# Sparse attention at the end of a two-block kernel: index scores computed during the projections, keys chosen beside the value projection, tiles 1 and 0 taken in turn

## The chip, the cores and the metric

One NeuronCore of a Trainium2 chip runs the whole program. The metric is the device time of one execution in microseconds; the median of the runs is compared. The engines are TensorE (PE), VectorE (DVE), ScalarE (ACT), GpSimd (POOL) and SyncE (SP), each with its own queue in order; they meet by semaphores alone.

## The reference

512 tokens of width 1024 go through a first block (gated linear attention, spatial gating, a mixture of experts) and a second one (a state-space mixer, a dense feed-forward, a sparse attention, a dense feed-forward, all in fp32). The change lies in the sparse attention:

```python
q, k, v, qi, ki, wi = split(h @ w_in)           # 16 heads of 64; 8 index heads of 64
q, k = rope(rmsnorm(q)), rope(rmsnorm(k))
qi, ki = rope(qi), rope(rmsnorm(ki))
for each block of 128 queries:
    score = sum over index heads of relu(qi @ ki.T) * wi      # causal
    sel   = the 128 keys of highest score
    out   = softmax(q @ k[sel].T / 8, causal) @ v[sel]
return out @ w_o
```

## The kernel before, in words

Activations stand transposed (features on the partitions, 512 tokens along a row) in pages of one large tile, `arena`. A product with an fp32 weight matrix is three products of split parts: `weights_high_part` (ACT, line 695) rounds half a chunk of weights, `weights_low_part` (DVE, line 703) forms the difference, two sets of parts take turns, and PE (`by_columns`, `by_rows`, line 336) waits for the set it needs. One half chunk holds the weights of one column block of 128. PE writes eight PSUM banks in the fixed order of the list `JOBS_B`; a bank is reused when its reader has freed it.

**Projections.** `ROPED` lists 21 column blocks of 128: eight of queries (`dq`), eight of keys (`dk`), four of index queries (`dqi`), one of index keys (`dki`); a loop of 23 steps walks them, and two value blocks (`dv`) stand in its last two steps. In step s PE makes `pr{s}` (24 products), the sum of squares `pn{s-1}` (line 1317) if that block is normed, and the rotary product `rot{s-2}` (line 1325). ACT squares and copies the block (1760, 1761), takes the root (1767) and rounds weights two blocks ahead. DVE inverts the root (2509), scales the block (2512), forms the weight difference, multiplies the rotary product by the sine (2525) and adds it to the block (2528), which POOL has multiplied by the cosine (906). The helper `copied` waits for its own instruction and then frees the bank; `link` waits for its own instruction alone.

**Attention.** `PAIRS` lists 64 pairs of a tile t of 128 queries and a head h, tile after tile; tile t sees (t + 1) x 128 keys. In step s PE makes the logits of pair s (line 1363), turns the probabilities of pair s-3 (1343, transposes) and multiplies those of pair s-4 with the values (1355). DVE adds the mask and takes the minimum (2582), and inverts the row sum (2539); ACT takes the exponential (1779), copies the turned probabilities (1789) and scales the outputs (1798, twice for two heads). In heads 1 to 4 of a tile, two index products a step of the next tile are added (1371), with a ReLU on ACT (1818) and a weighted sum on DVE (2559, 2562); POOL masks the diagonal (912). In heads 5 to 15 DVE chooses the next tile's keys: 16 rounds of `max` (eight largest) and `match_replace` (2597, 2598), and then the mask (2600). When a tile is done, eight transposes (1334) bring its rows back. The output projection (`wo`) waits for all tiles.

The order of the work is written out by hand: `JOBS_B` for PE and the banks, and the loops of each engine's program for the rest.

## Time and profile before

| | us |
|---|---|
| median of three runs | 3180.33 (3180.3 to 3219.16) |
| the profiled execution | 3193.29 |
| its span | 3191.5 |
| PE, DVE, ACT, POOL busy | 2930.1, 1876.4, 1406.8, 217.7 |

The span is the time between the first and the last instruction that the profiler saw on the core. Busy is the sum of an engine's instructions; a busy PE can run at either of two clocks, 1.2 or 2.4 GHz, which the profile gives as a granted share of 0.50 or 1.00. In the page's 40 slices of the span the granted clock is 0.6 and 0.5 in the two slices from 2633 to 2713 us, which lie in the attention. The last column of a group says which engine's work ended most of its idle time. The product of two fp32 operands is two instructions in the trace, a transpose one.

### The profile page before, as it was taken

How to read it: one execution, taken by the hardware profiler on the slowest of the kernel's cores; microseconds unless marked ns; L12 is line 12 of the kernel's file. 1: busy time of each engine (PE TensorE's matmuls, PEld its weight loads, DVE VectorE, ACT ScalarE, POOL GpSimd, SP SyncE). 2: the span in 40 equal slices, each digit the busy share in tenths (PEclk: the TensorE clock that was granted, in tenths of full speed). 3: DMA queues.
4: the chain of work that ended last, by engine and by line, in shares of the span. 5: the costliest groups of instructions: out<-in, count | busy, mean ns of one | idle time of the engine just before them, and what ended most of it. 6: DMA issues, size and time to landing. Idle time of an engine off the chain costs nothing.

```text
span 3191.5 us, 35348 instructions
## 1 busy us (share of the span) xinstructions
PE 2930.1 (92%) x12584; PEld 2247.2 (70%) x12584; DVE 1876.4 (59%) x2157; ACT 1406.8 (44%) x1858; POOL 217.7 (7%) x167
## 2 busy tenths in 40 slices
PE   7999999985899999999984678999989999989998
PEld 2548878765677777777773466888867766768887
DVE  3436643564988888888887754333249567343322
ACT  2323323223677777777775233222133344332321
POOL 1100100003930000000001000000001100000000
PEclk8999989995999999999997889999999965999999
DMA  6921722313898989899992812222221200112221
GB/s 229 331 76 60 288 75 93 111 65 150 319 344 354 387 354 387 352 387 352 387 360 74 106 43 76 93 103 96 93 74 67 79 27 1 37 69 99 99 93 66
DMA packets 90799, 546.88 MB, mean 171 GB/s; under 512 B 9232, under 2 KB 18848, under 8 KB 32384
## 3 DMA queue, kind: packets, MB, share of 16 engines
q1 hardware_dynamic: 79584, 485.65, 41.0%
q0 software_dynamic: 10816, 59.58, 5.4%
q8 instruction: 72, 1.18, 0.2%
q14 instruction: 39, 0.32, 0.0%
q10 hardware_dynamic: 288, 0.15, 0.0%
HBM read 516.51 MB, written 41.42 MB: 175 GB/s over the span
## 4 chain that ended last, share of the span: by engine, by line
PE 71%; DVE 15%; issue 6%; DMA 4%; ACT 3%; POOL 1%; SPq 1%; DVEq 0%; ACTq 0%; PEldq 0%; POOLq 0%
PE bank L336 39%; PE bank L274 6%; PE bank L1124 4%; PE bank L1128 4%; PE bank L1127 4%; DVE expert_low L2196 4%; PE bank L1363 2%; DMA arena<-in_we_stream 2%; PE bank L1355 1%; ACT expert_high L1559 1%; DMA arena<-in_mod 1%; PE bank L1343 1%; PE bank L1108 1%; DVE arena L2298 1%; DVE expert_x_low L2281 1%
## 5 line engine op out<-in xcount | busy, mean ns | idle before, releaser
L2196 DVE TENSOR_TENSOR expert_low<-arena,expert_high 128x2048 fp32r<-128x2048 f32 x291 | 683.4, 2379 | 102.3 <-ACT expert_high L1559 84.1
L1559 ACT ACTIVATE expert_high<-arena 128x1024 fp32r<-128x1024 f32 x582 | 596.9, 1057 | 212.3 <-PE bank L1124 120.5
L336 PE MATMUL bank<-high_b,weight_parts 128*128 128x512 f32 x1872 | 592.9, 398 | 30.4 <-DVE low_b L2434 16.2
L703 DVE TENSOR_TENSOR weight_parts<-ring_pages,weight_parts 128x1024 fp32r<-128x1024 f32 x185 | 226.9, 1227 | 556.0 <-ACT weight_parts L695 555.4
L695 ACT ACTIVATE weight_parts<-ring_pages 128x1024 fp32r<-128x1024 f32 x185 | 196.0, 1060 | 590.4 <-PE bank L336 547.0
L336 PEld LDWEIGHTS bank<-high_b,weight_parts 128*128 128x128 f32 x1872 | 352.5, 190 | 121.9 <-issue 37.2
L336 PE MATMUL bank<-low_b,weight_parts 128*128 128x512 f32 x832 | 324.8, 390 | 0.0
L1124 PE MATMUL bank<-expert_high,expert_x_low 128*128 128x512 f32 x768 | 309.4, 403 | 13.5 <-DVE expert_low L2196 9.9
L1127 PE MATMUL bank<-expert_high,expert_x_high 128*128 128x512 f32 x768 | 300.9, 392 | 0.0
L1128 PE MATMUL bank<-expert_low,expert_x_high 128*128 128x512 f32 x768 | 300.5, 391 | 0.0
L336 PE MATMUL bank<-hidden_parts,weight_parts 128*128 128x512 f32 x1056 | 240.0, 389 | 4.3 <-DVE hidden_parts L2480 4.3
L336 PEld LDWEIGHTS bank<-hidden_parts,weight_parts 128*128 128x128 f32 x1056 | 198.1, 188 | 46.3 <-DVE hidden_parts L2480 5.2
L336 PE MATMUL bank<-high_x,parts_a 128*128 128x512 f32 x640 | 204.6, 402 | 10.4 <-DVE parts_a L703 9.9
L1124 PEld LDWEIGHTS bank<-expert_high,expert_x_low 128*128 128x128 f32 x768 | 144.7, 188 | 68.3 <-DVE expert_low L2196 37.9
L336 PEld LDWEIGHTS bank<-low_b,weight_parts 128*128 128x128 f32 x832 | 156.8, 188 | 32.7
L1124 PE MATMUL bank<-expert_high,expert_h_low 128*128 128x512 f32 x384 | 156.2, 407 | 17.5 <-DVE expert_low L2196 15.1
L1128 PEld LDWEIGHTS bank<-expert_low,expert_x_high 128*128 128x128 f32 x768 | 144.8, 188 | 31.6
L1127 PEld LDWEIGHTS bank<-expert_high,expert_x_high 128*128 128x128 f32 x768 | 144.9, 189 | 28.0
L1128 PE MATMUL bank<-expert_low,expert_h_high 128*128 128x512 f32 x384 | 150.3, 391 | 0.0
L1127 PE MATMUL bank<-expert_high,expert_h_high 128*128 128x512 f32 x384 | 150.1, 391 | 0.0
L336 PEld LDWEIGHTS bank<-high_x,parts_a 128*128 128x128 f32 x640 | 123.2, 194 | 37.8 <-issue 11.1
L336 PE MATMUL bank<-high_b,parts_a 128*128 128x512 f32 x320 | 127.8, 399 | 0.0
(457 smaller groups left out, 4113.6 us busy)
## 6 DMA issues: line engine op xcount, KB each, us to landing
arena<-in_we_stream SPq DMA_DIRECT2D x294, 1024.0 KB, 6.4
ring_pages<-in_wb_stream SPq DMA_DIRECT2D x93, 1024.0 KB, 4.8
ring_pages<-in_wa_stream SPq DMA_DIRECT2D x49, 1024.0 KB, 4.8
arena<-in_mod POOLq DMA_DIRECT2D x16, 1024.0 KB, 6.7
xbuf<-arena POOLq DMA_DIRECT2D x25, 512.0 KB, 15.9
arena<-xbuf SPq DMA_DIRECT2D x17, 512.0 KB, 7.3
ybuf<-arena SPq DMA_DIRECT2D x16, 512.0 KB, 2.6
arena<-kd SPq DMA_DIRECT2D x8, 512.0 KB, 22.1
```

Of the source, the lines that this page charges most:

```text
L274: ins = pe.matmul(o, lhsT, rhs, start=start, stop=stop)
L336: ins = pe.matmul(o, lhsT, rhs, start=start, stop=stop)
L695: nc.scalar.activation(high, src, ACT.Copy).then_inc(weights_high, 1)
L703: nc.vector.tensor_tensor(low, src, high.bitcast(F32), ALU.subtract).then_inc(weights_split, 1)
L1108: ins = pe.transpose(ps[:, q * P:(q + 1) * P], parts[:, q * P:(q + 1) * P], ident[:])
L1124: ins = pe.matmul(o, low, w_high, start=start, stop=False)
L1127: pe.matmul(o, high, w_high, start=False, stop=False)
L1128: return pe.matmul(o, high, w_low, start=False, stop=stop)
L1343: ins = pe.transpose(ps[:, b * P:(b + 1) * P], pp[:, k % 4, b * P:(b + 1) * P], ident[:])
L1363: pe.matmul(ps[:, 0:(t + 1) * P], qT[r:r + 64, h // 2, t * P:(t + 1) * P], kT[r:r + 64, h // 2, 0:(t + 1) * P], start=True, stop=True).the ...
L1559: nc.scalar.activation(ehigh[c % HIGH_E][:, at], ring_e[c % RING_E][:, at], ACT.Copy) \
L2196: nc.vector.tensor_tensor(elow[c % RING_E][:], ring_e[c % RING_E], ehigh[c % HIGH_E][:].bitcast(F32), ALU.subtract).then_inc(weights_split ...
```

## The change

- `dqi` and `dki` come first in `ROPED` and in the weight stream. From step 8 (`INDEX_FIRST`) to step 19 each projection step has two index products behind `pr{s}`, two ReLUs on ACT ahead of the root, and two score instructions on DVE at the end of its step. The head weights (`wip`, `wi`) are made in steps 5 and 6. Scores of each tile stand in that tile's own `bias` page.
- DVE no longer adds the rotary parts; it writes the sine product to one of two pages (`rt`), and POOL does product and addition. POOL masks a tile's diagonal inside the same loop.
- The 48 rounds of choosing are spread: one in each of steps 13, 15, 17 and 19, sixteen and twelve beside the two value blocks (four or three behind each of four weight differences), and one in every third attention step up to step 47.
- `PAIRS` takes two heads of tile 1 and two of tile 0 in turn (numbers from 0), 32 steps, then tile 2, then tile 3. PE no longer waits for all rotated blocks before the first logits, but for the block that a pair needs.
- ACT no longer scales the outputs: DVE inverts two row sums at once and scales two heads in one instruction (`outputs_scaled`).
- In the first six attention steps PE makes one more product, `fill{s}`, whose result nobody reads, and waits for its end; before the first it waits for all value rows.

```diff
-            ("dq", "col", 0, 8), ("dk", "col", 0, 8), ("dqi", "col", 0, 4), ("dki", "col", 0, 1),
+            ("dqi", "col", 0, 4), ("dki", "col", 0, 1), ("dq", "col", 0, 8), ("dk", "col", 0, 8),
...
-ROPED = [("dq", j, True, 0) for j in range(KT)] + [("dk", j, True, 1) for j in range(KT)]
-ROPED += [("dqi", j, False, None) for j in range(4)] + [("dki", 0, True, None)]
+ROPED = [("dqi", j, False, None) for j in range(4)] + [("dki", 0, True, None)]
+INDEX_FIRST = len(ROPED) + 3
+ROPED += [("dq", j, True, 0) for j in range(KT)] + [("dk", j, True, 1) for j in range(KT)]
 NR = len(ROPED)
+INDEXED = [(t, i) for t in range(1, NTX) for i in range(IH)]
+
+
+def indexed_at(s):
+
+    return INDEXED[2 * (s - INDEX_FIRST):2 * (s - INDEX_FIRST) + 2] if s >= INDEX_FIRST else []
...
-PAIRS = [(t, h) for t in range(NTX) for h in range(AH)]
+assert sum(len(indexed_at(s)) for s in range(NR)) == len(INDEXED)
+
+PAIRS = []
+for _order in ((1, 0) * (AH // 2), (2,) * (AH // 2), (3,) * (AH // 2)):
+    for _n, _t in enumerate(_order):
+        PAIRS += [(_t, 2 * _order[:_n].count(_t) + i) for i in range(2)]
...
-NSTEP = NPAIR + MIX_LAG
...
+NSTEP, FILLED = NPAIR + MIX_LAG, 6
+TILE_DONE = {PAIRS.index((t, AH - 1)) + MIX_LAG: t for t in range(NTX)}
...
+            pool.wait_ge(S["b_bias0"], 1)
+            nc.gpsimd.affine_select(out=bias[0], in_=bias[0], compare_op=ALU.is_ge, fill=-MASKED, base=0,
+                                    pattern=[[-1, P]], channel_multiplier=1).then_inc(S["b_masked"], 1)
             for s in range(NR):
                 pool.wait_ge(bank_done, JB[f"rot{s}"] + 1)
                 v = roped_tile(s)
                 nc.gpsimd.tensor_tensor(v, v, cossin[:, 0, :], ALU.mult).then_inc(S["b_turned_cos"], 1)
-            pool.wait_ge(S["b_bias0"], 1)
-            nc.gpsimd.affine_select(out=bias[0][:, 0:P], in_=bias[0][:, 0:P], compare_op=ALU.is_ge, fill=-MASKED, base=0,
-                                    pattern=[[-1, P]], channel_multiplier=1).then_inc(S["b_masked"], 1)
-            for t in range(1, NTX):
-                pool.wait_ge(S["b_score_ready"], t)
-                nc.gpsimd.affine_select(out=score[:, t * P:(t + 1) * P], in_=score[:, t * P:(t + 1) * P],
-                                        compare_op=ALU.is_ge, fill=MASKED, base=0, pattern=[[-1, P]],
-                                        channel_multiplier=1).then_inc(S["b_masked"], 1)
+                pool.wait_ge(S["b_turned_cos"], s + 1)
+                pool.wait_ge(S["b_turned_sin"], s + 1)
+                nc.gpsimd.tensor_tensor(v, v, rt[:, s % 2, :], ALU.add).then_inc(S["b_rotated"], 1)
+                for t in range(1, NTX):
+                    if s < NR and (t, IH - 1) in indexed_at(s):
+                        pool.wait_ge(S["b_score_ready"], t)
+                        diagonal = bias[t][:, t * P:(t + 1) * P]
+                        nc.gpsimd.affine_select(out=diagonal, in_=diagonal, compare_op=ALU.is_ge, fill=MASKED, base=0,
+                                                pattern=[[-1, P]], channel_multiplier=1).then_inc(S["b_masked"], 1)
...
+                    for n, (t, i) in enumerate(indexed_at(s)):
+                        if s == INDEX_FIRST and n == 0:
+                            pe.wait_ge(S["b_rotated"], INDEX_FIRST - 3)
+                        ps = opened(f"ix{t}{i}")
+                        r = 64 * (i % 2)
+                        pe.matmul(ps[:, 0:(t + 1) * P], qiT[r:r + 64, i // 2, t * P:(t + 1) * P],
+                                  kiT[r:r + 64, 0:(t + 1) * P], start=True, stop=True).then_inc(bank_done, 1)
+                    if s == 5:
...
-            pe.wait_ge(S["b_rotated"], 2 * KT)
...
+                    pe.wait_ge(S["b_rotated"], NR - KT + h // 2 + 1)
...
-                    if t < NTX - 1:
-                        if s == 1:
-                            pe.wait_ge(S["b_rotated"], NR)
-                        for i in index_heads(h):
-                            ps = opened(f"ix{t + 1}{i}")
-                            r = 64 * (i % 2)
-                            pe.matmul(ps[:, 0:(t + 2) * P], qiT[r:r + 64, i // 2, (t + 1) * P:(t + 2) * P],
-                                      kiT[r:r + 64, 0:(t + 2) * P], start=True, stop=True).then_inc(bank_done, 1)
+                if s < FILLED:
+                    if s == 0:
+                        pe.wait_ge(S["b_v_rows"], 2 * NTX)
+                    ps = opened(f"fill{s}")
+                    pe.matmul(ps[:], ident[:], vt[:, 0, 0:512], start=True, stop=True).then_inc(bank_done, 1)
+                    pe.wait_ge(bank_done, JB[f"fill{s}"] + 1)
+                    pe.sem_inc(free(f"fill{s}"), 1)
...
+                    for t, i in indexed_at(s):
+                        ps = result(act, f"ix{t}{i}")
+                        if n_relu >= 2:
+                            act.wait_ge(relu_used, n_relu - 1)
+                        n_relu += 1
+                        copied(act, nc.scalar.activation(rl[:, i % 2, 0:(t + 1) * P], ps[:, 0:(t + 1) * P],
+                                                         ACT.Relu), S["b_relu_ready"], n_relu, f"ix{t}{i}")
...
-                if VALUE_LAG <= s < NPAIR + VALUE_LAG and (s - VALUE_LAG) % 2 == 1:
-                    k = s - VALUE_LAG
-                    name = f"av{k - 1}"
-                    act.wait_ge(av_done, k // 2 + 1)
-                    act.wait_ge(S["b_sums_ready"], k + 1)
-                    for n in (k - 1, k):
-                        t, h = PAIRS[n]
-                        ins = nc.scalar.activation(mixed_rows[t % 2][:, h * HD:(h + 1) * HD],
-                                                   psum[JB[name] % 8][:, h % 2 * HD:(h % 2 + 1) * HD], ACT.Copy,
-                                                   scale=rsm[:, n % 8:n % 8 + 1])
-                        ins.then_inc(S["b_o_ready"], 1)
-                    act.wait_ge(S["b_o_ready"], k + 1)
-                    act.sem_inc(free(name), 1)
...
+            def index_score(t, i):
+
+                n = IH * (t - 1) + i + 1
+                w = (t + 1) * P
+                dve.wait_ge(S["b_relu_ready"], n)
+                if i == 0:
+                    ins = nc.vector.tensor_scalar(bias[t], rl[:, i % 2, 0:w], wi[:, t, i:i + 1], None, ALU.mult)
+                else:
+                    ins = nc.vector.scalar_tensor_tensor(out=bias[t], in0=rl[:, i % 2, 0:w], scalar=wi[:, t, i:i + 1],
+                                                         in1=bias[t], op0=ALU.mult, op1=ALU.add)
+                ins.then_inc(relu_used, 1)
+                dve.wait_ge(relu_used, n)
+                if i == IH - 1:
+                    dve.sem_inc(S["b_score_ready"], 1)
+
+            chosen = [0]
+
+            def choose(n):
+
+                for _ in range(n):
+                    t, at = 1 + chosen[0] // (TOPK // 8), chosen[0] % (TOPK // 8)
+                    if t == NTX:
+                        return
+                    chosen[0] += 1
+                    if at == 0:
+                        dve.wait_ge(S["b_masked"], t + 1)
+                    link(nc.vector.max(m8[:], bias[t]))
+                    link(nc.vector.match_replace(bias[t], m8[:], bias[t], TAKEN))
+                    if at == TOPK // 8 - 1:
+                        link(nc.vector.tensor_scalar(bias[t], bias[t], TAKEN / 2, -MASKED, ALU.is_gt, ALU.mult))
+
             for s in range(NR + 2):
-                if s == NR + 1:
-                    ps = result(dve, "wi")
-                    link(nc.vector.tensor_scalar(wi, ps[:, 0:NTX * IH].rearrange("p (t h) -> p t h", h=IH),
-                                                 float(IH) ** -0.5, float(HD) ** -0.5, ALU.mult, ALU.mult))
-                    dve.sem_inc(free("wi"), 1)
                 if s >= NR:
-                    weights_low_part(dve, half_of("dv", s - NR, KT, True) + 1, split_to)
+                    for q in range(4):
+                        weights_low_part(dve, half_of("dv", s - NR, KT, True) - 2 + q, split_to)
+                        choose(4 if s == NR else 3)
...
+                    if s >= 4:
+                        dve.wait_ge(S["b_rotated"], s - 3)
+                    copied(dve, nc.vector.tensor_tensor(rt[:, s % 2, :], ps[:], cossin[:, 1, :], ALU.mult),
+                           S["b_turned_sin"], s - 1, name)
...
+                    for t, i in indexed_at(s):
+                        index_score(t, i)
+                    if s >= INDEX_FIRST + 5 and s % 2:
+                        choose(1)
...
+            def outputs_scaled(k):
+
+                t, h = PAIRS[k - 1]
+                name = f"av{k - 1}"
+                dve.wait_ge(S["b_exped"], k + 1)
+                link(nc.vector.reciprocal(rsm[:], sm[:, (k - 1) % 8:k % 8 + 1]))
+                dve.wait_ge(av_done, k // 2 + 1)
+                copied(dve, nc.vector.tensor_tensor(
+                    mixed_rows[t][:, h * HD:(h + 2) * HD].rearrange("p (h d) -> p h d", h=2),
+                    psum[JB[name] % 8][:, 0:2 * HD].rearrange("p (h d) -> p h d", h=2),
+                    rsm[:].unsqueeze(2).to_broadcast([P, 2, HD]), ALU.mult), S["b_o_ready"], k // 2 + 1, name)
...
+                if VALUE_LAG <= s < NPAIR + VALUE_LAG and (s - VALUE_LAG) % 2 == 1:
+                    outputs_scaled(s - VALUE_LAG)
+                if s in TILE_DONE:
+                    mixed_low(TILE_DONE[s])
+                if s < 3 * AH and s % 3 == 2:
+                    choose(1)
```

## Rows read from the trace of the kernel before

**Rows 1.** Stretches of the timeline: attention by tile, busy time of each engine, granted clock

```profile
2567.20:2598.00 30.80, 24.08 (x90) 15.94 (x88) 23.29 (x96) 17.03 (x64) 1.85 (x3) 0.65 0.05 22
2598.00:2646.30 48.30, 48.30 (x150) 31.86 (x151) 35.67 (x116) 24.03 (x79) 0.29 (x1) 0.50 0.00 1
2646.30:2700.70 54.40, 52.55 (x191) 33.79 (x189) 40.06 (x107) 27.00 (x74) 0.29 (x1) 0.63 0.00 1
2700.70:2749.60 48.90, 48.90 (x213) 31.83 (x214) 16.56 (x52) 24.30 (x63) 0.00 (x0) 0.77 0.00 1
2749.60:2758.90 9.30, 6.46 (x53) 5.72 (x53) 2.41 (x6) 4.88 (x13) 0.00 (x0) 1.00 0.00 0
```

**Rows 2.** The chain of waits in the projections: start, length, engine, line, pieces

```profile
2476.20 5.49 PE bank L336 x24
2481.69 0.86 PE bank L1317 x2
2482.55 0.86 PE bank L1325 x2
...
2521.54 21.79 PE bank L336 x96
```

**Rows 3.** Timeline of VectorE in one projection step: start, length, line, what

```profile
2469.36 3.35 DVE L2509 RECIPROCAL arena<-arena 128x512 f32<-128x512 f32 x1 [0.36 <-ACT arena L1767]
...
2473.53 1.23 DVE L703 TENSOR_TENSOR weight_parts<-ring_pages,weight_parts 128x1024 fp32r<-128x1024 f32 x1
2474.90 0.69 DVE L2525 TENSOR_TENSOR arena<-bank,arena 128x512 f32<-128x512 f32 x1
2475.74 0.69 DVE L2528 TENSOR_TENSOR arena<-arena 128x512 f32<-128x512 f32 x1
```

**Rows 4.** Groups of instructions in the attention: busy, mean ns, idle before, releaser

```profile
L1818 ACT ACTIVATE arena<-bank 128x512 f32<-128x512 f32 x8 | 4.8, 597 | 4.9 <-PE bank L1371 4.4 <-ACT arena L1818 0.4 <-ACT arena L1798 0.2
...
L2597 DVE MAX8 m<-arena 128x8 f32<-128x512 f32 x16 | 10.9, 682 | 0.3
...
L2562 DVE SCALAR_TENSOR_TENSOR arena<-arena 128x512 f32<-128x512 f32 x7 | 5.3, 752 | 2.4 <-ACT arena L1818 2.1
```

**Rows 5.** Groups of instructions in the projections: square root, GpSimd's product

```profile
L1767 ACT ACTIVATE arena<-bank,eps 128x512 f32<-128x512 f32 x17 | 11.7, 687 | 3.0 <-ACT arena L1761 2.2 <-PE bank L1317 0.5
...
L906 POOL TENSOR_TENSOR arena<-arena 128x512 f32<-128x512 f32 x20 | 26.6, 1330 | 170.7 <-PE bank L1325 170.7
```

**Rows 6.** Timeline of VectorE in tiles 0 and 1: logits and the next instruction

```profile
2580.74 0.29 DVE L2582 CUSTOM_DVE_ANT_0 arena<-bank,arena 128x128 f32<-128x128 f32 x1 [0.20 <-DVE arena L2598]
...
2581.19 0.16 DVE L2539 RECIPROCAL rsm<-sm 128x1 f32<-128x1 f32 x1
...
2621.25 0.42 DVE L2582 CUSTOM_DVE_ANT_0 arena<-bank,arena 128x256 f32<-128x256 f32 x1
...
2621.90 0.16 DVE L2539 RECIPROCAL rsm<-sm 128x1 f32<-128x1 f32 x1 [0.21 <-DVE nmx L2582]
```

**Rows 7.** Timelines of VectorE and GpSimd where they meet

```profile
2498.39 1.56 DVE L703 TENSOR_TENSOR weight_parts<-ring_pages,weight_parts 128x1024 fp32r<-128x1024 f32 x1 [0.67 <-ACT weight_parts L695]
...
2497.04 1.83 POOL L906 TENSOR_TENSOR arena<-arena 128x512 f32<-128x512 f32 x1 [5.04 <-PE bank L1325]
```

**Rows 8.** Stretches of tiles 1, 2 and 3, logit products alone: count, clock

```profile
2615.80:2643.30 27.50, 13.42 (x22) 5.49 (x22) 0.50 0.00 1
2673.00:2700.00 27.00, 12.12 (x15) 3.49 (x14) 0.50 0.00 1
2725.40:2749.80 24.40, 11.23 (x20) 2.94 (x20) 1.00 0.00 1
```

**Rows 9.** Timeline of PE: the last tile turned back

```profile
2755.91 1.09 PE L1334 MATMUL bank<-ident,arena 128*128 128x128 f32 x8 [0.61 <-ACT arena L1798]
```

**Rows 10.** Two stretches of 4 us at the high clock

```profile
2668.00:2672.00 4.00, 2.84 (x19) 1.98 (x17) 3.65 (x10) 1.60 (x5) 0.00 (x0) 1.00 0.00 0
2756.00:2760.00 4.00, 2.12 (x13) 1.71 (x14) 1.38 (x2) 1.61 (x3) 0.00 (x0) 1.00 0.00 0
```

More of the change, by code:

```diff
@@ L170 @@
         JOBS_B += [f"lg{_s}"]
-        if PAIRS[_s][0] < NTX - 1:
-            JOBS_B += [f"ix{PAIRS[_s][0] + 1}{i}" for i in index_heads(PAIRS[_s][1])]
+    if _s < FILLED:
+        JOBS_B += [f"fill{_s}"]
 JOBS_B += [f"wo{j}" for j in range(KT)] + ["sn4"]
@@ L641, in block_kernel @@
         cossin = page(31, 2, T)
-        bias = [page(32, T), page(43, T)]
-        score = page(32.5, T)
-        rl = page(33, 2, T)
+        bias = [page(first, (t + 1) * P) for t, first in enumerate((32, 37.75, 32.125, 32.5))]
+        rl = page(36, 2, T)
         pp = page(34, 4, T)
         pT = page(36, 2, T)
-        wi_rows = page(36.5, T)
+        wi_rows = page(34, T)
         rope = page(37.5, P)
         half1 = page(37.625, P)
-        mixed_rows = [page(42, D), page(43.5, D)]
+        mixed_rows = [page(first, D) for first in (42, 43.5, 42, 43.5)]
         sqt = page(42, 2, T)
         rst = page(43, 2, T)
-        rt = page(44, 1, T)
-        m8, nmx, sm, rsm = (sb(n, [P, k]) for n, k in (("m8", 8), ("nmx", 4), ("sm", 4), ("rsm", 8)))
+        rt = page(33, 2, T)
+        m8, nmx, sm, rsm = (sb(n, [P, k]) for n, k in (("m8", 8), ("nmx", 4), ("sm", 8), ("rsm", 2)))
         for n in ("sq_full", "h_full", "s5_in", "u_made", "u2_copied", "coef_exp", "coef_ready", "cp_ready", "qb_ready",
@@ new lines, in _ @@
+                    if s == 5:
+                        ps = opened("wip")
+                        pe.wait_ge(S["small_operands"], 3)
+                        for kt in range(KT):
+                            for w, h in ((0, low_p), (0, high_b), (1, high_b)):
+                                ins = pe.matmul(ps[0:IH, :], wi_parts[:, w, kt, :], h[:, kt, :],
+                                                start=(kt == 0 and h is low_p), stop=(kt == KT - 1 and w == 1))
+                        ins.then_inc(bank_done, 1)
@@ L1312, in _ @@
+                    if s == 6:
+                        ps = opened("wi")
+                        pe.wait_ge(S["small_operands"], 4)
+                        for t in range(NTX):
+                            ins = pe.transpose(ps[:, t * IH:(t + 1) * IH], wi_rows[0:IH, t * P:(t + 1) * P],
+                                               ident[0:IH, 0:IH])
+                        ins.then_inc(bank_done, 1)
+                else:
                     by_rows([f"dv{s - NR}{t}" for t in range(NTX)], ("dv", s - NR),
@@ L2548, in mixed_low @@
                                             high_b[:, at[0], at[1]].bitcast(F32), ALU.subtract).then_inc(split_ready, 1)
[L2549 removed]
+                    dve.wait_ge(split_ready, 3 * KT + FFT + n_mixed[0])
                     dve.sem_inc(free(name), 1)
[L2552 to L2572 removed]
             for s in range(NSTEP):
```

130 lines of the change are left out of this document (35 added, 95 removed).

## Prediction

> **What bounds the kernel now.** The change touches two stages of the second block: the projections (which end near 2567 us of the span) and the attention behind them. The stretches of the timeline by stage come first [rows 1]. From 2567.2 to 2758.9 the attention takes 191.7 us: 30.8 for tile 0, 48.3 for tile 1, 54.4 for tile 2, 48.9 for tile 3, and 9.3 for the last pairs. The reader is to see two things: PE is busy for nearly all of it, and its granted clock is 0.50 to 0.65 over the first three tiles, so most of this "busy" is the low level of 1.2 GHz. By the logit products a step took 2.5 us in tile 1 and 3.6 in tile 2 at 0.50, but 2.44 in tile 3 at 1.00, although tile 3 is the widest [rows 8] (two products a step; tile 2 shows 15 for 7.5 steps). What the clock does is worth more than any instruction here.
>
> The chain of waits shows the projections: a step is 5.49 us of weight products and two fp32 products of 0.86, a period of 7.2 us, all PE [rows 2]. The timeline of VectorE has the second thing to see: from one reciprocal's start to the end of the sine product it needs 6.23 us, and with the addition behind it nearly fills the 7.2 [rows 3]. VectorE is hidden, but barely.
>
> **The change, part by part.**
>
> *Index scores into the projections.* Steps 8 to 19 each get two index products on PE, two ReLUs on ScalarE ahead of the square root, and two score instructions on VectorE behind the sine product. On PE a pair uses both halves of the rows; I take 0.47, 0.7 and 0.9 us for widths of 256, 384 and 512, from the 0.86 of a 512-wide fp32 product [rows 2]: 4 x 2.07 = 8.3 us in twelve steps. If PE alone counted, that would be all.
>
> It does not. The two ReLU buffers close a ring: the second ReLU of step s+1 waits until VectorE has used the second one of step s; the square root is queued behind that ReLU; the reciprocal waits for the root; and behind the reciprocal stand the scores of step s+1. Round the ring at width 512: 6.23 from reciprocal to sine product, 0.15 to the next instruction [rows 3], two scores of 0.75, ReLU 0.60 [rows 4], square root 0.69 [rows 5], and 0.37 of handovers (0.1 to ScalarE, 0.17 between two of its instructions, 0.1 back; estimates from the gaps of the 7.2 us period): 9.54 us. At width 256 each score takes some 0.27 less (0.13 for 128 columns, as the logits show [rows 6]) and a ReLU some 0.22 less: 8.8, and 9.2 between them. PE can do such a step in 7.7 to 8.1. The step of choosing in every second step runs beside ReLU and root and adds nothing.
>
> *GpSimd's addition.* It takes one VectorE instruction of 0.69 us off each step (counted above), and puts one of 1.33 [rows 5] on GpSimd at the very moment VectorE begins the scores. The trace shows what two such do to each other: GpSimd's product beside a VectorE addition took 1.83 us where its mean is 1.33, and the weight difference that began while it still ran took 1.56 instead of 1.23 [rows 7, 3, 5]. 0.48 of overlap cost 0.33, so a whole overlap of some 1.3 costs 0 to 1.3; I take 1.1 a step, by that ratio with a margin for full blocking. The Trainium skill (SBUF — State Buffer, Who interferes with whom) says that a VectorE instruction with two SBUF inputs and a GpSimd instruction that reads SBUF exclude each other for the whole instruction; the score instructions have two such inputs, so by it the full 1.3 would be paid. The two stretched rows agree in direction.
>
> So eleven periods from step 8 to step 19: 3 x 8.8 + 4 x 9.2 + 4 x 9.54 = 101.3, plus 11 x 1.1 = 113.4 us. In step 8 the weight difference is ready 8.6 us after that step's products end (7.5 before, plus two narrow ReLUs); the value products need the one made in step 19, so they start at 8.6 + 113.4 = 122.0. Before, this took 1.72 + 12 x 7.2 = 88.1. Cost: 34 us. Bounds: 8 (PE alone) and 36.
>
> *Choosing beside the value projection.* A value block is 21.8 us in four parts of 5.45 [rows 2]. VectorE comes to it 4.6 us behind, with the reciprocal of step 19 still to do, so the second part's weights are ready 10 us after the start: PE waits 4.5. Then a part costs VectorE 1.23 for the weights and four rounds of 0.96 (256 wide, so twice 0.41, with the load and gaps), 5.1 in all, just under 5.45; 0.6 is lost at the first of them. The last four rounds (384 wide, 1.3 each) and the last reciprocal push the first weights of block two to 9.3 us after its start, where 5.45 are given: 3.9. Together 9 us; bounds 0 and 13. The projections cost 34 + 9 = **+43 us**, between 8 and 49. Index weights first, and the head weights' products at steps 5 and 6, only reorder equal work: 0, hidden under PE's own work; if VectorE were late there too, under 1 us.
>
> *The attention without scores and choosing.* Six steps hold a filler of 0.86 (the same shape as the rotary product [rows 2]) plus its own wait, some 0.2, on top of about 0.6 of pair work: 1.65 x 6 = 9.9. VectorE's lag at the start, 2 to 3 us, lies under the first three fillers, and the first logits no longer wait for all keys. In the other 26 paired steps PE needs at the high clock half of the 2.5 for tile 1 [rows 8] and about 0.75 for tile 0, 1.0 on average. VectorE needs more: from logits to the next instruction 0.65 (width 256) or 0.45 (width 128) [rows 6]; the scaled outputs, now here instead of two ScalarE copies, 0.16 + 0.29 + two waits of 0.15 = 0.75 for two steps (no row shows this instruction; between 0.5 and 1.0, taken as a 128-wide one out of PSUM [rows 6]); a round of choosing 512 wide, twice 0.68 with a short load and gaps, 1.5, in every third step [rows 4]. Sum 0.55 + 0.37 + 0.51 = 1.43 x 26 = 37.2. Tile 2 at the high clock is PE's: between half of its 3.6 and three quarters of tile 3's 2.44 [rows 8], with some fixed cost 1.9, x 16 = 30.4. Tile 3: 16 x 2.44 = 39.0. Three tiles turned back at 1.1 [rows 9] = 3.3, start 1.0, end 9.3 [rows 1]. Sum **130.1**, against 191.7: **-61.6 us**, if the clock stays high.
>
> Net -61.6 + 43 = -19 us. The profiled execution took 3193.3 us for a span of 3191.5 and is 13.0 above the median of 3180.3; I carry the difference over to the median: 3161 us, in the profile 3174.
>
> **Does the clock stay high?** It fell in tile 2 after a stretch in which PE was busy 2.84 of 4 us, and at the end of the attention it stayed at 1.00 through 2.12 of 4 [rows 10]. The paired steps leave PE some 70% busy, between the two, with holes of up to 1.7 us where choosing and scaling fall together. The trace does not settle it. The Trainium skill (TensorE: Matmul & The Clock Gate, Why this matters for your kernels) says that it is long idle gaps between bursts of products that throw the clock back. By it the high level would hold and the time is 3161; the fall in tile 2, with 1.16 of 4 us idle [rows 10], speaks against it.
>
> **The rivals.**
> 1. *Clock falls in the paired steps, for good until tile 3* (slower). After the fillers, four steps more at 1.43, then 22 at 2.0: 1.0 + 9.9 + 5.7 + 44 = 60.6; tile 2 16 x 3.6 = 57.6 and 3.8 for two tiles turned back; tile 3 48.9; end 9.3: 180 us. -11.5 + 43 = +31: 3211. For it: dense steps of tiles 1 and 2 never brought the clock back before [rows 8]. Against: six fillers bridge the start, where it fell before. It decides once the 22 steps (0.57 each, 12.5 us) and four of tile 2 (1.7 each) are at the low level: 19 us.
> 2. *It falls, and comes back at the start of tile 2*, where two tiles are turned back close together, as it did in tile 3: 60.6 + 3 + 30.4 + 3.3 + 39 + 9.3 = 146, -46 + 43: 3177.
> 3. *The ring is not paid*: PE stays the bound of the projections, +8.3 and 3 or 4 in the value blocks, with a high clock: -50: 3130. For it: VectorE lost 0.84 a step. Against: the sum round the ring.
>
> **How the numbers follow.** Forecast 0.40, alone 3140 to 3178 (its upper end: slower scaling and full blocking; its lower: no blocking, -12). Rival 1 0.22, rival 2 0.17, rival 3 0.13, 0.04 beyond each end. Range 3122 to 3214, which leaves out less than 2 in 10. Two per cent is 64 us, about what can be told from no change. Faster by more (below 3117) needs rival 3 and a cheaper attention yet: 0.05. Slower by more (above 3244) needs rival 1 and stalls beyond all bounds: 0.04. Within: 0.91.
>
> **What would show it.** Projections: idle PE ahead of weight products, ended by VectorE's weight difference, some 2.5 us in steps 10 to 20; a period near 10 us instead of 8; score instructions near 1.9 us for the first of a pair; GpSimd's additions at 1.3. Value blocks: waits of 4 to 5 and 4 us. Attention: clock rows at 1.00 from 2600 on, paired steps of 1.4 us, tile 2 at 1.9. Wrong would be: ReLUs that never wait for a score, or a clock of 0.50 in tile 2.

## The result and the profile after

The kernel after took 3220.59 us (median of 20 runs, 3213.14 to 3230.18), the kernel before 3211.05 us beside it (median of 20 runs, 3180.30 to 3223.83): a ratio of 1.0058, 95% interval 1.0033 to 1.0083. That is 9.5 us slower, less than 2%. The forecast was 3161, 19 us faster than before, in a range that ended at 3214; the measured time is 6.6 us beyond that end.

The runs of before have two groups, 3180 to 3191 and 3210 to 3224. The median of three that I started from, and the profiled execution (3193.29), belong to or lie near the lower one. The 9.5 us are a comparison with a mixture: in the 20 runs beside it, nine are of the lower group (median 3185.55) and eleven of the upper (3219.16), so the kernel after is 35.0 us slower than the one and 1.4 slower than the other. So before was profiled once more, as a kernel of its own (c4 below). The stretches of the kernel after and of this second profile follow: projections (first rotary product to first logit product), attention (to the first output-projection product), and the rest. Columns: window, length, busy time and count of PE, PE's weight loads, VectorE, ScalarE, GpSimd, then the granted clock, the DMA share and GB/s. The kernel after:

```profile
2378.50:2610.40 231.90, 207.06 (x777) 139.81 (x775) 183.55 (x199) 75.19 (x112) 56.92 (x43) 0.96 0.17 60
2610.40:2784.40 174.00, 167.62 (x653) 111.27 (x652) 78.04 (x255) 68.84 (x201) 2.53 (x2) 0.69 0.01 5
2784.40:3218.60 434.20, 415.65 (x1792) 338.22 (x1792) 142.84 (x150) 114.54 (x136) 0.00 (x0) 0.98 0.24 85
```

The kernel before, its second profile:

```profile
2378.60:2558.10 179.50, 179.50 (x726) 132.96 (x724) 125.02 (x100) 61.84 (x84) 26.58 (x20) 1.00 0.23 81
2558.10:2777.80 219.70, 207.30 (x690) 137.05 (x689) 118.08 (x374) 96.49 (x289) 2.43 (x5) 0.56 0.01 2
2777.80:3212.20 434.40, 415.03 (x1792) 337.76 (x1792) 142.82 (x150) 114.54 (x136) 0.00 (x0) 0.98 0.24 85
```

Against this profile the projections took 52.4 us more and the attention 45.7 less: +6.7, and the spans differ by 6.4. Against the first profile of before the projections give the same +52.4 (179.5 again), but the attention, there 190.7 by the same marks, gives only -16.7. There the projections had also begun 10.2 us later, and the rest was 1.6 us shorter; the edit lies in neither, and the reason stays open. (52.4 - 16.7 - 10.2 + 1.6 = 27.1 is the difference of the two spans.) Three lessons stand in these six rows. The projections' price is the same in both pairs of profiles. The attention's price hangs on which execution is profiled: the same code of before took 190.7 and 219.7 us, at a mean clock of 0.65 and 0.56. And the last rows agree within 0.2, so between these two profiles nothing else moved.

**The projections after.** The timelines of VectorE, ScalarE and GpSimd over one period (start, length, line, what; in brackets the idle time before it and what ended it), to be held against [rows 3, 5, 7]:

```profile
2503.48 3.35 DVE L2547 RECIPROCAL arena<-arena 128x512 f32<-128x512 f32 x1 [1.55 <-ACT arena L1798]
2506.87 0.75 DVE L2550 SCALAR_TENSOR_TENSOR arena<-arena,cols 128x512 f32<-128x512 f32 x1
2507.66 1.22 DVE L714 TENSOR_TENSOR weight_parts<-ring_pages,weight_parts 128x1024 fp32r<-128x1024 f32 x1
2509.09 0.69 DVE L2562 TENSOR_TENSOR arena<-bank,arena 128x512 f32<-128x512 f32 x1 [0.21 <-DVE weight_parts L714]
2509.93 3.24 DVE L2516 SCALAR_TENSOR_TENSOR arena<-arena 128x384 f32<-128x384 f32 x2
...
2514.82 3.35 DVE L2547 RECIPROCAL arena<-arena 128x512 f32<-128x512 f32 x1 [0.56 <-ACT arena L1798]
...
2511.71 0.60 ACT L1787 ACTIVATE arena<-bank 128x512 f32<-128x512 f32 x1 [6.18 <-DVE arena L2516]
2513.26 0.60 ACT L1787 ACTIVATE arena<-bank 128x512 f32<-128x512 f32 x1 [0.96 <-DVE arena L2516]
2514.03 0.69 ACT L1798 ACTIVATE arena<-bank,eps 128x512 f32<-128x512 f32 x1 [0.17 <-ACT arena L1787]
...
2509.93 1.27 POOL L923 TENSOR_TENSOR arena<-arena 128x512 f32<-128x512 f32 x1 [8.41 <-DVE arena L2562]
2511.16 1.59 POOL L920 TENSOR_TENSOR arena<-arena 128x512 f32<-128x512 f32 x1
```

The ring is there as predicted: the ReLU waits for a score, the root stands behind the ReLU, the reciprocal waits for the root. This period is 11.34 us, the eleven 10.9 on average. The two scores take 3.24 us for the two together, where 2.3 was forecast. GpSimd shows why: right behind the addition (L923) comes the cosine product (L920) of the next block, and the two together lie over both scores. The eleven periods, PE idle for a sixth of them:

```profile
2439.00:2559.40 120.40, 100.74 (x353) 62.20 (x352) 102.96 (x79) 41.59 (x65) 32.46 (x24) 0.96 0.15 53
```

In the table of waits over the projections (engine and line, waited for what: us in total, times, longest) the ring is the second row, the first that is shown; PE's own idle time ends at the rotary product (L1348), which waits for the normed rows, and only then at the weights (L714):

```profile
ACT arena L1787 <- DVE arena L2516: 55.7, 19, 6.3
...
PE bank L1348 <- DVE arena L2550: 17.2, 10, 3.4
DVE arena L2547 <- ACT arena L1798: 16.2, 12, 1.9
...
PE bank L348 <- DVE weight_parts L714: 7.4, 12, 3.7
```

One more row belongs to the value blocks. PE waited 3.71 us for the second part's weights, until 2564.81, and then worked at 1.2 GHz for 6 us:

```profile
2565.00:2571.00 6.00, 6.00 (x15) 4.70 (x16) 5.43 (x15) 1.06 (x1) 1.28 (x1) 0.50 0.02 4
```

From the first value product to the first logit product it is 56.6 us here and 46.8 in the second profile of before, where PE is busy all the time at 1.00:

```profile
2553.80:2610.40 56.60, 51.41 (x198) 40.19 (x198) 53.10 (x102) 13.96 (x17) 8.17 (x6) 0.91 0.24 81
```

**The attention after**, by the granted clock: six steps with fillers, a few paired steps at the high level, then the fall; a return in tile 2, a second fall, and the return in tile 3. This answers to [rows 1, 8, 10]:

```profile
2610.40:2624.40 14.00, 12.20 (x41) 5.47 (x41) 7.08 (x24) 5.86 (x17) 2.53 (x2) 1.00 0.12 52
2624.40:2629.70 5.30, 5.01 (x27) 3.57 (x26) 3.64 (x14) 2.43 (x10) 0.00 (x0) 0.93 0.00 0
2629.70:2682.00 52.30, 51.85 (x163) 35.38 (x163) 27.78 (x103) 19.33 (x76) 0.00 (x0) 0.50 0.00 1
2682.00:2694.00 12.00, 10.91 (x61) 7.83 (x60) 7.01 (x18) 6.38 (x16) 0.00 (x0) 0.93 0.00 0
2694.00:2745.00 51.00, 51.00 (x153) 32.84 (x152) 17.71 (x55) 15.80 (x42) 0.00 (x0) 0.50 0.00 1
2745.00:2784.40 39.40, 36.65 (x215) 26.18 (x214) 14.83 (x44) 19.04 (x42) 0.00 (x0) 0.96 0.00 1
```

103 of the 174 us ran at 1.2 GHz. The same stage's logit products alone give the length of a step (two of the counted products are one step):

```profile
2631.80:2670.30 38.50, 19.33 (x38) 9.48 (x38) 0.50 0.00 1
2698.20:2723.20 25.00, 11.49 (x14) 3.46 (x14) 0.50 0.00 1
2751.90:2774.30 22.40, 10.07 (x18) 2.65 (x18) 1.00 0.00 1
```

So a paired step took 2.03 us at the low level (1.33 in the four steps from 2624.4 to 2629.7, mostly at the high one), a step of tile 2 3.57, and one of tile 3 2.49 at the high level.

### The profile page after: what moved, and what is told of

The parts are those of the page before. It is cut to its first block, busy times and chain, and to the rows that moved or that the text cites. A ratio compares the mean times of both kernels' runs of the same rounds, so it can differ in the third digit from the quotient of the medians.

```text
span 3218.6 us, 35358 instructions
## 1 busy us (share of the span) xinstructions
PE 2947.3 (92%) x12596; PEld 2246.9 (70%) x12596; DVE 1892.0 (59%) x2136; ACT 1390.6 (43%) x1794; POOL 248.9 (8%) x188
## 4 chain that ended last, share of the span: by engine, by line
PE 67%; DVE 19%; issue 6%; ACT 4%; DMA 3%; SPq 1%; DVEq 0%; POOL 0%; ACTq 0%; POOLq 0%; PEldq 0%
PE bank L348 37%; PE bank L286 6%; PE bank L1139 4%; PE bank L1143 4%; PE bank L1142 4%; DVE expert_low L2203 4%; DMA arena<-in_we_stream 2%; PE bank L1386 2%; DVE arena L2547 1%; PE bank L1377 1%; ACT expert_high L1581 1%; DVE arena L2516 1%; PE bank L1365 1%; PE bank L1123 1%; DVE expert_x_low L2288 1%
## 5 line engine op out<-in xcount | busy, mean ns | idle before, releaser
L714 DVE TENSOR_TENSOR weight_parts<-ring_pages,weight_parts 128x1024 fp32r<-128x1024 f32 x185 | 226.7, 1226 | 538.7 <-ACT weight_parts L706 537.8
```

The lines of the kernel that those rows point to most:

```text
L714: nc.vector.tensor_tensor(low, src, high.bitcast(F32), ALU.subtract).then_inc(weights_split, 1)
```

## Experiments

Two theories of the projections: the ring of two ReLU buffers (ring theory), and the blocking of VectorE by GpSimd, both of which read SBUF (port theory). Two of the attention: its length is the clock's history (clock theory); or VectorE's choosing and scaling bind it. All ratios are against before on the same chip. They move with the mixture of before's two groups: its upper group has 13 of 31 runs beside a1 to a4, 11 of 16 beside b1 to b4, and 14 of 31 beside c1 to c4. So a3 (3180.66 us) has a ratio of 0.9958 and b2 (3183.11 us) one of 0.9897, and ratios of different letters are not to be compared. All ratios lie within 2%.

**a1: square root ahead of the ReLUs.**

```diff
 # ScalarE, step s
-    (two ReLUs of step s)
     square root of step s - 1
     high part of the weights of step s
+    (two ReLUs of step s)
```

> The changed kernel with ScalarE's two ReLUs moved behind the square root and the weight rounding of the same step; nothing else. Ring theory (the root queued behind a ReLU that waits for a score closes the period): VectorE's reciprocal no longer idles before it starts (0.6 to 1.7 us a step in the changed kernel), the period of steps 9 to 19 falls from 10.3 to 11.4 us by that idle time, about 1 us a step, 10 to 15 us in all. Port theory (GpSimd's two instructions stretch the two scores): scores stay at 3.3 us a pair, and the period cannot fall under VectorE's own work, 3.35 + 0.75 + 1.22 + 0.69 + 3.3 + gaps = 9.8 us. Rival, PE or the weights bound the period: no change.

3203.88 us (10 runs), ratio 1.0014, 0.9969 to 1.0059. The projections fell from 231.9 to 218.3 us; the eleven periods:

```profile
2438.10:2546.40 108.30, 100.64 (x372) 64.14 (x370) 103.25 (x79) 43.02 (x67) 33.74 (x25) 0.98 0.17 59
```

VectorE is as busy as before the edit (103), but its reciprocals no longer wait: their idle time before them fell from 11.5 to 0.5 us in the same 140 us. The attention was 174.0 again, with the same history of the clock. The ring is shown, with a price of 13.6 us (10 to 15 expected), 12.1 of it in the eleven periods.

**a2: the addition back on VectorE.**

```diff
 # GpSimd
-    wait turned_sin; v = v + rt        (then_inc rotated)
 # VectorE, behind the sine product
+    wait turned_cos; v = v + rt        (then_inc rotated)
```

> The changed kernel with the addition of the rotary parts back on VectorE; GpSimd keeps the cosine product. Port theory: the pair of scores falls from 3.3 us to 1.1 (width 256) to 1.5 (width 512), VectorE gains an instruction of 0.84 with its gap, so a period falls by about 1 us, 10 to 13 us in twelve steps. Ring theory alone (no blocking, the scores are slow for a reason of their own): the period grows by 0.84 us a step, 10 us slower.

3217.73 us (11 runs), ratio 1.0055, 1.0015 to 1.0095. Projections 225.5 in the profile, 6.4 less (8.1 in the eleven periods), although VectorE has one more instruction of 0.69 a step. 10 to 13 us were expected: the direction is the port theory's, the gain is smaller than forecast. The groups of the score instructions (count, busy, mean ns) show it, first of the kernel after, in 2460 to 2600:

```profile
L2516 DVE SCALAR_TENSOR_TENSOR arena<-arena 128x512 f32<-128x512 f32 x7 | 11.2, 1606 | 0.6
L2516 DVE SCALAR_TENSOR_TENSOR arena<-arena 128x384 f32<-128x384 f32 x7 | 10.3, 1470 | 0.6
```

and of a2:

```profile
L2513 DVE SCALAR_TENSOR_TENSOR arena<-arena 128x512 f32<-128x512 f32 x7 | 5.3, 752 | 0.2
L2513 DVE SCALAR_TENSOR_TENSOR arena<-arena 128x384 f32<-128x384 f32 x7 | 4.3, 618 | 0.2
```

0.85 us on each score, 1.7 on each step. The ring is still there: the reciprocals idle for 11.8 us in the same 140. The profiled execution had an attention of 157.6, where the kernel after, with the same code in that stage, had 174.0. It took 3197.64 us, 17 less than the next fastest of its runs (3214.43), so its attention is not that of the median.

**a3: both edits.**

> Both: ReLUs behind the root, addition on VectorE. If ring and port together are the cause, the period of steps 9 to 19 is VectorE's own work, 3.35 + 0.75 + 1.22 + 0.69 + 0.69 + 1.1 to 1.5 + half a round of choosing 0.5 + gaps 0.5 = 8.8 to 9.2 us or PE's 7.7 to 8.1 where choosing is absent: 20 us less than the changed kernel over the projections, so about 3200 us, near the kernel before. If something else bounds the projections, less than the sum of the two runs alone.

3180.66 us (10 runs), ratio 0.9958, 0.9916 to 1.0000. Projections 210.4; attention 152.6 in this execution.

```profile
2437.40:2536.50 99.10, 95.83 (x369) 63.03 (x368) 93.85 (x90) 42.47 (x67) 17.20 (x14) 1.00 0.19 64
2380.00:2590.40 210.40, 198.82 (x778) 137.88 (x776) 179.42 (x222) 75.19 (x112) 27.83 (x23) 0.98 0.19 68
2590.40:2743.00 152.60, 144.91 (x653) 96.72 (x652) 78.74 (x253) 69.01 (x201) 1.26 (x1) 0.81 0.01 3
2682.50:2696.80 14.30, 14.00 (x78) 9.28 (x77) 9.59 (x29) 7.22 (x21) 0.00 (x0) 1.00 0.01 2
```

The two prices add up: 13.6 + 6.4 = 20.0 singly, 21.5 together (20 expected). The stage is still 30.9 us longer than before: 99.1 against eleven of 7.2 (79.2) in the periods, the rest in the value blocks and at their ends. Both engines are nearly full in the first row, 95.8 and 93.9 of 99.1. The last row is seven steps of tile 2 at the high level, 2.04 us each.

**a4: the kernel after without its six fillers** (`FILLED = 0`).

> The changed kernel without the six filler products. If the fillers only delay the fall of the clock by their own length: the first six paired steps fall from 2.0 to 1.3 us or so, the granted clock falls 8 us earlier, and the time is 0 to 4 us less. If they hold the clock up to some use: the paired steps at 1.9 to 2.0 come earlier and the time is up to 5 us more. The return of the clock in tile 2 for 10 us, and in tile 3, stays in both.

3203.41 us (10 runs), ratio 1.0034, 0.9991 to 1.0077. The clock fell 5 us into the attention (19 with fillers), and it came back 73 us into it in both kernels, so the fillers cost what their 14 us at the high level gave. The attention still took only 156.4 (0 to 4 us less than 174.0 were expected), since here the clock then stayed for 34 us, not 10, and was away for some 14 us instead of 54. Holding the clock for the first steps is not what sets the length.

**b1, b2, b3: a3 without fillers, with a product written into each logit product's own bank ahead of it**, in the first three tiles: 256 columns wide, none, and 512 wide. Its result is overwritten. Before the first, PE also waits for the value rows (left out below).

```diff
     ps = opened(f"lg{s}")
+    if s < 48:
+        pe.matmul(ps[:, 0:256], ident[:], vt[:, 0, 0:256], start=True, stop=True)
     (the logit product)
```

> The kernel of a3_both, with the six filler products replaced by one 256 wide (0.43 us at the high clock) ahead of each logit product of the steps 0 to 47, in that product's own bank, so that nothing waits for it. Clock theory (the attention's time is the granted clock's doing): the clock stays at 1.00 through all tiles, paired steps take VectorE's 1.4 to 1.5 us, tile 2 about 2.3, tile 3 2.45; attention 1 + 32 x 1.45 + 16 x 2.3 + 39 + 3 + 9 = 135 us against 152.6 in a3_both; time about 3165. Rival (the clock falls all the same, since the narrow steps are too thin even so): paired steps at 0.50 become 0.85 longer, 2.8 us, and the attention takes 170 or more.

> The kernel of a3_both without any filler product. If six fillers only put off the fall: attention as in a3_both less 0 to 4 us, some 150 us, unless the return in tile 2 fails, which costs up to 27 more (16 steps of 3.6 instead of 1.9).

> As b1_thin_48 with fillers 512 wide (0.86 us at the high clock) in the steps 0 to 47. The clock stays at 1.00 surely; paired steps become PE's, 1.0 + 0.9 = 1.9 us, tile 2 2.75: attention 1 + 61 + 44 + 39 + 3 + 9 = 157 us. If b1 keeps the clock too, b3 is slower than it by some 20 us; if b1 loses it, b3 is faster than b1.

b1: 3187.41 us (4 runs: 3168.60, 3175.79, 3199.03, 3202.30), ratio 0.9896, 0.9824 to 0.9968. b2: 3183.11 (4 runs), 0.9897, 0.9845 to 0.9950. b3: 3184.17 (7 runs), 0.9901, 0.9872 to 0.9929. The profiled execution of b1, first paired steps, then tile 2, then tile 3:

```profile
2585.50:2637.90 52.40, 50.15 (x253) 31.56 (x252) 33.32 (x119) 23.11 (x89) 0.73 (x1) 1.00 0.00 1
2640.70:2680.20 39.50, 38.80 (x209) 24.83 (x208) 22.48 (x67) 18.36 (x50) 0.00 (x0) 1.00 0.00 1
2704.40:2746.20 41.80, 41.80 (x127) 27.23 (x126) 8.76 (x27) 11.67 (x27) 0.00 (x0) 0.50 0.00 1
```

The added product kept 2.4 GHz through the paired steps and tile 2, and then the clock fell and tile 3 took 4.6 us a step (nine in 41.8) instead of 2.49. So the attention took 176.0 us, where 135 was expected. That one fall is 16 x 2.1 = 34 us, and the kernel's four runs are 34 us apart, at mean clocks of 0.955 and 0.960 in the two faster and 0.946 and 0.948 in the two slower; that the faster ones kept the clock in tile 3 fits, but they were not profiled. In b2 the clock fell at once and came back in tile 2 (attention 157.7, some 150 expected). In b3 it was 1.00 from end to end:

```profile
2588.10:2746.80 158.70, 154.72 (x735) 88.26 (x734) 77.68 (x252) 67.46 (x201) 0.33 (x1) 1.00 0.00 1
```

158.7 us at the full clock (157 expected), 4 of it idle: the 512-wide products cost what the clock gives.

**b4: the kernel before with the 256-wide product in its first three tiles.**

> The kernel before, with a filler 256 wide ahead of each logit product of the steps 0 to 47 (tiles 0 to 2), in its own bank. Clock theory: clock 1.00 through the attention; tile 0 and 1 become VectorE's (choosing in most steps: 1.8 and 2.6 us a step), tile 2 2.4 to 2.6, tile 3 2.45: attention 3 + 29 + 42 + 41 + 39 + 13 = 167 us against 191 (and against 160 to 191 in other executions), so some 20 us off the time, with less spread. Rival (scores and choosing of VectorE set the attention before, not the clock): 191 stays or grows.

3224.91 us (10 runs), ratio 1.0020, 0.9973 to 1.0067. The clock fell 22 us in, came back twice and stood at 0.50 for the last 112 us; attention 233.8, where 167 was expected. The added product alone does not hold the clock. Nor does VectorE bind the stage, as the rival had it: it is busy for 117.5 of the 233.8 us, PE for 225.1.

**c1: as b1, in all four tiles.**

> The kernel with the square root first and the addition on VectorE, no separate fillers, and a 256-wide product ahead of every logit product of all four tiles. Clock theory: what decides the attention is at which of the two levels it runs; with the thin product in the first three tiles alone the clock held 1.00 until the end of tile 2 and then fell, so with it in tile 3 too it holds to the end. Then the attention takes 176.0 less the low part (tile 3 at 0.50 took some 27 us more than at 1.00) plus 16 x 0.2 of added products, some 150 us, and the span is 3171. Rival, fall by chance: the fall does not hang on what the product fills; then it falls in tile 2 or 3 again, attention 170 to 180, span 3195.

3177.69 us (10 runs, 3166.88 to 3183.91; before 3188.64), ratio 0.9915, 0.9878 to 0.9951: 0.85% less than before, and 7.4 us less than the median of before's lower group there (3185.13). The spread of 17 us leaves no room for a run with all of tile 3 at the low level, which costs some 34; the profiled run (3183.58), one of the slowest, had it at 1.00. The profiled execution, split at a short fall:

```profile
2592.70:2645.20 52.50, 50.23 (x253) 31.56 (x252) 33.42 (x119) 23.11 (x89) 0.73 (x1) 1.00 0.00 1
2645.20:2662.00 16.80, 15.67 (x57) 9.74 (x56) 6.51 (x23) 6.63 (x20) 0.00 (x0) 0.70 0.00 0
2662.00:2747.50 85.50, 82.43 (x460) 53.77 (x458) 38.16 (x112) 37.91 (x92) 0.00 (x0) 1.00 0.00 1
```

Attention 154.8, near the 150 expected, but the clock was away for 10 us at the start of tile 2, so the product makes the high level likelier and not sure. Expected span 3171, profiled 3181.7.

**c2: a3 with the tiles in their old order.**

```diff
-for _order in ((1, 0) * (AH // 2), (2,) * (AH // 2), (3,) * (AH // 2)):
+for _order in ((0,) * (AH // 2), (1,) * (AH // 2), (2,) * (AH // 2), (3,) * (AH // 2)):
```

> The kernel with the square root first and the addition on VectorE, with the tiles in their old order (0, 1, 2, 3) instead of the first two alternating; all else the same. Theory that the order is what spares VectorE: tile 0 alone costs PE less than VectorE's 1.4 us a step, tile 1 alone more, so the pair loses up to 16 x 0.2 us, attention 153 to 160. Rival, the order matters through the clock alone: the dense steps of tile 1 lie together, the clock comes back at another place than with the tiles alternating, and the attention moves by 10 us or more either way.

3183.74 us (10 runs), ratio 0.9963, 0.9916 to 1.0011; a3's ratio was 0.9958. Attention 155.8 (a3 152.6; 153 to 160 expected). The alternation is worth nothing that can be told here.

**c3: a3 without fillers, the 512-wide product in tiles 2 and 3 alone.**

> The kernel with the square root first and the addition on VectorE, no separate fillers, and a 512-wide product ahead of the logit product in tiles 2 and 3 alone. Clock theory: the paired steps run at 0.50 and are bound by the products at that level, some 62 us; a denser tile 2 keeps the clock once it is back. Return theory: it comes back in tile 2 as it does without the products, attention 158 plus up to 32 x 0.21 = 165 us. Rival, dense work holds the clock down: with more products it stays at 0.50 through tile 2, 32 us more, 190 us.

3209.43 us (10 runs), ratio 1.0038, 0.9998 to 1.0078. Attention 180.8, where 165 was expected. Paired steps, the start of tile 2, the rest:

```profile
2585.50:2650.00 64.50, 60.46 (x200) 42.56 (x200) 35.62 (x126) 25.26 (x95) 1.26 (x1) 0.54 0.01 5
2650.00:2666.00 16.00, 16.00 (x35) 7.16 (x33) 3.61 (x11) 4.02 (x11) 0.00 (x0) 0.50 0.00 0
2666.00:2766.30 100.30, 96.85 (x473) 55.41 (x472) 39.53 (x116) 39.09 (x95) 0.00 (x0) 1.00 0.00 1
```

The clock came back in tile 2, as the return theory had it; a PE busy for 16.00 of 16 us at the low level did not keep it there, as the rival had it. The price was wrong: the added products cost more than the 0.21 us each that I had put down. Against b2 (157.7) the stage is 23.1 us longer, 0.7 for each of 32, although b2 was at the low level for some 10 us more; at the high level a step of tile 2 took 2.92 us (twelve in 35.0) against 2.04 in a3, so each product costs its full length on PE.

**c4: before, unchanged.**

> The kernel before, unchanged, profiled once more. Theory that its two groups of times (3180 to 3191, 3210 to 3224) are two histories of the clock in the attention: a profile of a run of the upper group shows an attention some 25 us longer with the clock at 0.50 in tile 3 or more of it, all other stages within 3 us. Rival, the groups come from elsewhere (transfers, the first block): the attention is 191 again and another stage differs.

3202.05 us (10 runs), ratio 0.9975, 0.9926 to 1.0024, with five runs at 3180 to 3190 and five at 3214 to 3218. The profiled one took 3214.06 us; its attention is 219.7, 29.0 more than in the first profile, and the stretch that covers most of tile 3 stands at the low level:

```profile
2721.00:2763.00 42.00, 42.00 (x127) 27.29 (x127) 7.77 (x27) 14.24 (x37) 0.00 (x0) 0.50 0.00 1
```

The first profile had 1.00 there [rows 8]. The mean clock of each of the ten runs tells the same: 0.936 to 0.941 in the lower group, 0.928 to 0.931 in the upper (0.938 in the first profile). So the two groups differ in the history of the clock, by one profile of each and the mean clock of all. One part of the expectation failed: another stage differs too, by the 10.2 us ahead of the projections, so the first profile took 3193 us and not 3183.

## Why the prediction was wrong, point by point

**The step that failed** is "-61.6 us, if the clock stays high", with the question behind it, "Does the clock stay high?". It did not. It held over the fillers and four steps more, fell, came back for 12 us in tile 2, and fell again. The rows of before had shown such a return: 1.00 in tile 2 at 2668 [rows 10], after 0.50 in tile 1 [rows 1], and a fall soon after. The prediction's own sign of being wrong, a clock of 0.50 in tile 2, is the row that starts at 2694. The return seen before also answers the reason given for rival 1, that the dense steps of tiles 1 and 2 never brought the clock back. The prices at either level were nearly right: a paired step 1.33 (forecast 1.43) and at the low level 2.03 (2.0); tile 2 2.04 in a3 (1.9) and 3.57 (3.6); tile 3 2.49 (2.44). Only the fillers were dear: six steps took 14.0 us, not 9.9, as each costs 1.1 on PE, 0.3 of waiting and its pair's work. With these prices all at the high level the stage would be 14.0 + 26 x 1.33 + 16 x 2.04 + 16 x 2.49 + 12.6 for turning tiles and the end = 133.7 us (worked out, not run). It took 174.0: the clock's price is some 40 us. No version ran it at 134: where added products held 2.4 GHz (b3, and c1 but for 10 us), they themselves cost most of the difference.

**The argument from [rows 10] was no argument.** I put 70% busy between 2.84 of 4 us, after which it fell, and 2.12 of 4, where it held. The fall came here while PE was busier than that:

```profile
2622.00:2626.00 4.00, 3.70 (x17) 2.16 (x17) 2.73 (x10) 1.20 (x5) 0.00 (x0) 1.00 0.00 0
2626.00:2630.00 4.00, 3.71 (x19) 2.59 (x18) 2.63 (x10) 1.97 (x9) 0.00 (x0) 0.87 0.00 0
```

The busy time of a row does not tell whether the clock holds. The rule quoted from the Trainium skill (TensorE: Matmul & The Clock Gate, Why this matters for your kernels), that long idle gaps throw the clock back, fits the 3.71 us wait in the value block and the 6 us at 0.50 behind it; it does not fit the fall at 2630, with no such gap ahead of it.

**The base.** The attention's -61.6 was counted from a profile with a good history (190.7). Over the two histories of before the changed kernel gains 16.7 or 45.7 us in the attention, where the forecast was 61.6. By mechanism the outcome lies between rival 1 (180 us, low until tile 3) and rival 2 (146, back at the start of tile 2), and by the total it is rival 1's sign with a larger bill in the projections. The second fall, after the return in tile 2, stood in neither.

**The projections: +52.4 us, forecast +43 between 8 and 49.** The price lies beyond the stated bound too. Of the 9.4 us between the two, some 7.0 are the eleven periods and 0.8 the value blocks; the last 1.6 were not traced further. The parts follow.

**The ring: right.** Eleven periods took 120.4, forecast 113.4. a1 shows the ring itself. PE's idle time lay ahead of the rotary product more than ahead of the weights, where I had looked for it.

**GpSimd's port: right in kind, mis-sized.** 1.1 us a step was forecast for the addition. The cosine product that follows it blocks the second score as well; a2 measures 1.7. The 0.6 a step between them make 6.6 of the 7.0 us by which the periods exceed the sum. By the Trainium skill (SBUF — State Buffer, Who interferes with whom) the two exclude each other for the whole instruction: scores of 0.62 and 0.75 became 1.47 and 1.61 beside products of 1.3 to 1.6, so the trace agrees; I had applied it to the moved instruction and not to its neighbour in the queue.

**The floor of 8 us was out of reach.** With ring and port gone (a3) the stage still costs 30.9. From the reciprocal to the addition VectorE took 7.1 of each 7.2 us [rows 3]; scores and choosing lift it to 8.5 (93.9 in eleven periods), and PE to 8.7.

**The value blocks: right in the sum, by luck.** 9 us of waiting were forecast, and the blocks cost 9.8 (56.6 against 46.8). But only 5.2 of it is waiting: 3.71 in the first block (forecast 4.5 and 0.6) and 1.47 in the second (3.9); the other 2.2 us in the table lie in the periods. The rest is the low clock behind two waits, that of 3.71 us and one of 3.42 for the last rotary product ahead of the blocks, a term that I had left out.

**Choosing and scaling in the attention** do not bind it: VectorE is busy for 78 of 174 us, and at the low level PE is busy for 51.85 of 52.3. The outputs' scaling costs 0.17 + 0.29, as forecast.

**Open** stays what makes the clock fall and return. In the eight profiles whose paired steps carry no added product (after, a1 to a4, b2, c2, c3) it was low for most of them; in the three with one in the changed kernel (b1, b3, c1) it held. Yet b4 fell with it, and the same code gave attentions of 174.0, 174.0 and 157.6 us (after, a1, a2). One regularity stands in the traces and was not tested. In the kernel after and its eight variants in which the clock fell and came back (a1 to a4, b2, c1 to c3), each of the 15 returns came within 3 us of the end of the eight transposes that turn a finished tile back. In the kernel after these are the two sets that ran at the low level:

```profile
2681.25 1.97 PE L1356 MATMUL bank<-ident,arena 128*128 128x128 f32 x8
2745.70 1.97 PE L1356 MATMUL bank<-ident,arena 128*128 128x128 f32 x8
```

Rival 2 had put the return there. But a set at the low level does not always bring it back: in b1 the clock stayed at 0.50 behind this one,

```profile
2695.41 1.97 PE L1353 MATMUL bank<-ident,arena 128*128 128x128 f32 x8
```

and in the two profiles of before and the one of b4 only three of six returns lie at such a set. No run changed the transposes alone, so a cause is not shown. Why the runs of after show one group and those of before two was not settled either.

## What to carry to other kernels

Before a sum is made against a profile in which the granted clock moves, profile the kernel twice and price the stage at each level; if the same code differs by more than the change is to bring, the clock's history is the forecast, and a chance of it is all that one can give. Work that is moved under a "hidden" engine needs that engine's slack per step (here 0.1 us of 7.2), and its buffers tie the engines into a ring, which a longer distance, such as the root ahead of the ReLUs, opens. When an instruction moves to GpSimd, its neighbours in GpSimd's queue move in time too: count them all against what VectorE does there.

## What the runs showed of the hardware

- Histories of the clock repeat. Counted from the start of the attention, the clock came back, fell and came back at 73, 83.5 and 138 us in after and a1 (174.0 us both), and at 73 to 74.5, 108 and 121 to 122 us in a2, a4 and b2 (157.6, 156.4 and 157.7 us), with fillers and without.
- A low clock can last with PE always busy: 42.00 of 42 us in c4, 41.80 of 41.8 in b1, 51.00 of 51 in the kernel after; and it can end under such a load (c3, 16.00 of 16).
- A VectorE instruction with one SBUF input and a scalar is stretched beside GpSimd too: the first score of tile 3, a product of 512 columns, took 1.58 us; in a2, where GpSimd's addition is gone, it took 0.49. The piece of the chain of waits:

```profile
2520.97 1.58 DVE arena L2514
```
